# Stick-breaking stage: key parts in tile order, query rows turned between key blocks, head norms and head turns by halves

## The reference, cut to what matters

```python
k, v = split(rms_norm_2(h, kv_norm) @ w_kv)         # 256 x 1024 each, 8 heads of 128
k = rms_norm_2(k, k_norm)                           # per head of 128
q = rms_norm_2(rms_norm_2(h, ln_mix) @ w_q, q_norm) * 128 ** -0.5
z = q @ k.T                                         # per head, keys before the query only
A[t, s] = sigmoid(z[t, s]) * prod(1 - sigmoid(z[t, j]) for s < j < t)
h = h + (A @ v) @ w_out
```

## Time and profile before

| what | value |
|---|---|
| median of 3 runs | 1352.71 us (1350.2 to 1352.77) |
| the profiled execution | 1354.37 us, span 1352.7 us |
| TensorE busy | 1283.1 us, 95% of the span |
| DVE busy | 766.8 us, 57% |
| ACT busy | 610.7 us, 45% |
| POOL busy | 77.6 us, 6% |
| DMA | 212.26 MB, 157 GB/s over the span |

### The profile page before, as it was taken

One profiled execution on the slowest core, in us unless ns is written; L12 is line 12 of the kernel. 1 busy time (PEld: TensorE's weight loads), 2 busy tenths in 40 slices (PEclk: granted clock), 3 DMA queues, 4 the chain that ended last, 5 costly groups with the idle time before them and its releaser, 6 DMA issues.

```text
span 1352.7 us, 16268 instructions
## 1 busy us (share of the span) xinstructions
PE 1283.1 (95%) x6667; PEld 1086.9 (80%) x6667; DVE 766.8 (57%) x852; ACT 610.7 (45%) x743; POOL 77.6 (6%) x125
## 2 busy tenths in 40 slices
PE   8999999988999998999799999999979889999997
PEld 6888888987788887999598788888768777888886
DVE  4655436974655545587874655544656516554444
ACT  5444336644444434556303544442545735444323
POOL 1000002001100002001101100000102001000001
PEclk9999999989999998999898999999989899999999
DMA  8865546330765562645100576554545315665530
GB/s 267 266 188 187 201 151 215 133 102 12 237 186 188 187 218 94 218 145 183 32 1 1 155 221 201 173 189 159 183 144 191 99 38 166 215 201 177 189 133 31
DMA packets 140138, 212.26 MB, mean 157 GB/s; under 512 B 10233, under 2 KB 101245, under 8 KB 140060
## 3 DMA queue, kind: packets, MB, share of 16 engines
q1 hardware_dynamic: 140064, 211.22, 48.0%
HBM read 210.14 MB, written 1.05 MB: 156 GB/s over the span
## 4 chain that ended last, share of the span: by engine, by line
PE 87%; DVE 6%; ACT 3%; issue 1%; POOL 1%; DMA 0%; SPq 0%; ACTq 0%; DVEq 0%
PE bank L1443 25%; PE bank L1445 25%; PE bank L1444 25%; DVE wlo L959 2%; PE bank L1819 2%; PE bank L1466 1%; PE bank L1568 1%; PE bank L1827 1%; DVE xTlo L980 1%; PE bank L1686 1%; PE bank L1835 1%; DVE X L1003 1%; ACT whi L375 1%; ACT xThi L396 1%; DVE y L1204 1%
## 5 line engine op out<-in xcount | busy, mean ns | idle before, releaser
L959 DVE TENSOR_TENSOR wlo<-raw,whi 128x2048 fp32r<-128x2048 f32 x190 | 434.1, 2291 | 295.9 <-ACT whi L375 295.7
L375 ACT ACTIVATE whi<-raw 128x2048 fp32r<-128x2048 f32 x190 | 362.1, 1913 | 227.0 <-PE bank L1445 219.7
L1443 PE MATMUL bank<-whi,xThi 128*128 128x512 f32 x1024 | 408.8, 399 | 20.9 <-DVE xTlo L980 8.8
L1445 PE MATMUL bank<-whi,xTlo 128*128 128x512 f32 x1024 | 402.2, 393 | 0.0
L1444 PE MATMUL bank<-wlo,xThi 128*128 128x512 f32 x1024 | 401.9, 393 | 0.0
L1443 PEld LDWEIGHTS bank<-whi,xThi 128*128 128x128 f32 x1024 | 194.4, 190 | 66.1 <-DVE xTlo L980 9.4
L1445 PEld LDWEIGHTS bank<-whi,xTlo 128*128 128x128 f32 x1024 | 194.1, 190 | 41.5
L1444 PEld LDWEIGHTS bank<-wlo,xThi 128*128 128x128 f32 x1024 | 194.6, 190 | 38.7
L1443 PE MATMUL bank<-whi,hThi 128*128 128x512 f32 x352 | 138.1, 392 | 0.0
L1445 PE MATMUL bank<-whi,hTlo 128*128 128x512 f32 x352 | 137.1, 390 | 0.0
L1444 PE MATMUL bank<-wlo,hThi 128*128 128x512 f32 x352 | 137.0, 389 | 0.0
(11 more groups left out here) (375 smaller groups left out, 1222.6 us busy)
## 6 DMA issues: line engine op xcount, KB each, us to landing
raw<-in_ffn_w_dram SPq DMA_DIRECT2D x176, 256.0 KB, 4.0
raw<-in_ffn_w_in_dram SPq DMA_DIRECT2D x176, 256.0 KB, 3.9
raw<-in_ffn_w_dram SPq DMA_DIRECT2D x22, 1024.0 KB, 5.0
raw<-in_ffn_w_out_dram SPq DMA_DIRECT2D x22, 1024.0 KB, 4.9
raw<-in_gdn_w_in_dram SPq DMA_DIRECT2D x16, 1024.0 KB, 5.4
raw<-in_w_in_dram SPq DMA_DIRECT2D x10, 1024.0 KB, 5.2
raw<-in_ple_w_gate_dram SPq DMA_DIRECT2D x8, 1024.0 KB, 5.0
raw<-in_w_kv_dram SPq DMA_DIRECT2D x8, 1024.0 KB, 6.3
```

Of the source, the lines that this page charges most:

```text
L375: act.activation(whi[w % SPLIT][:], raw[w % RAW][:], ACT.Copy).then_inc(w_hi, 1)
L959: dve.tensor_tensor(wlo[w % SPLIT][:], raw[w % RAW][:], whi[w % SPLIT][:].bitcast(F32), ALU.subtract).then_inc(w_lo, 1)
L1443: pe.matmul(psum, lhs[0], rhs[0], start=start, stop=False, skip_group_check=True)
L1445: return pe.matmul(psum, lhs[1], rhs[0], start=False, stop=stop, skip_group_check=True)
```

## The change

`ahead` becomes 4 for "kv". TensorE does the four key slots on the first tile (n7's second turn before the last of them), then on the second tile, with the two turns of n8 before the third and the fourth part. DVE scales both tiles for n8 straight after n7. Squares, sums, roots and head norms are done for a half (512 columns, four heads) of both tiles as soon as the half is there; `sq_s` is used in two parts. Head turns go by halves too: both key halves before query block s+6, the first query half before s+8, the second after it. Bank 4 takes the first tile's turn and bank 5 the second's, where it was the half. Splits are placed anew between these steps. The computation is unchanged. The diff, with repeated signatures left out:

```diff
@@ -258,7 +258,7 @@
             arrived.append(total[w % RAW])
 
         def ahead(follows):
-            return {"up1": 3, "up2": 3, "up3": 3, "ple_g0": 4, "ple_g1": 4}.get(follows, 2)
+            return {"up1": 3, "up2": 3, "up3": 3, "ple_g0": 4, "kv": 4, "ple_g1": 4}.get(follows, 2)
 
         FIRST, PIECES = 2, 4
 
@@ -686,19 +686,19 @@
                                              ACT.Copy)
                     ins.then_inc(sem("s_kqv"), 1)
 
-                def squares(i):
+                def squares(i, b):
                     for t in range(NT):
-                        if 2 * i + t:
-                            act.wait_ge(sem("s_kss"), 2 * i + t)
-                        act.wait_ge(sem("s_kqv"), 2 * i + 2)
-                        act.activation(sq_s[:], kn[:, t, :], ACT.Square).then_inc(sem("s_sq"), 1)
-
-                def turned_heads(i, dst):
+                        n = 4 * i + 2 * b + t
+                        if n >= 2:
+                            act.wait_ge(sem("s_kss"), n - 1)
+                        act.wait_ge(sem("s_kqv"), 2 * i + b + 1)
+                        act.activation(sq_s[:, t * 512:(t + 1) * 512], kn[:, t, b * 512:(b + 1) * 512], ACT.Square).then_inc(sem("s_sq"), 1)
+
+                def turned_heads(i, b, dst):
                     for t in range(NT):
-                        for b in range(2):
-                            act.wait_ge(sem("s_kT"), 4 * i + 2 * t + b + 1)
-                            act.activation(dst[:, 4 * b:4 * b + 4, t * P:(t + 1) * P],
-                                           bank[4 + b][:].rearrange("p (k c) -> p k c", k=4), ACT.Copy).then_inc(sem("s_kT_in"), 1)
+                        act.wait_ge(sem("s_kT"), 4 * i + 2 * b + t + 1)
+                        act.activation(dst[:, 4 * b:4 * b + 4, t * P:(t + 1) * P],
+                                       bank[4 + t][:].rearrange("p (k c) -> p k c", k=4), ACT.Copy).then_inc(sem("s_kT_in"), 1)
 
                 def exp_abs(heads):
                     for h in heads:
@@ -720,30 +720,34 @@
 
                 norm(7, WIDE.index("ple_g0"), "kv", before=gate)
                 split(s + 1 + SPLIT)
+                turn_hi("n8", 0, xThi2)
                 act.wait_ge(w_used, s + 2)
                 evacuate(0, kn)
                 split(s + 2 + SPLIT)
-                norm(8, WIDE.index("ple_g0"), None, xThi2)
+                turn_hi("n8", 1, xThi2)
+                squares(0, 0)
                 split(s + 3 + SPLIT)
                 act.wait_ge(w_used, s + 4)
                 evacuate(1, kn)
-                split(s + 4 + SPLIT)
-                squares(0)
+                squares(0, 1)
                 split(s + 5 + SPLIT)
                 act.wait_ge(w_used, s + 6)
                 act.wait_ge(sem("s_rows"), 2)
                 evacuate(2, kn)
+                squares(1, 0)
+                for b in range(2):
+                    turned_heads(0, b, skT)
                 split(s + 7 + SPLIT)
                 act.wait_ge(w_used, s + 8)
+                act.wait_ge(sem("s_rows"), 4)
                 evacuate(3, kn)
-                turned_heads(0, skT)
-                split(s + 8 + SPLIT)
-                squares(1)
+                squares(1, 1)
+                turned_heads(1, 0, sqT)
                 split(s + 9 + SPLIT)
                 act.wait_ge(w_used, s + 10)
                 evacuate(4, vs)
+                turned_heads(1, 1, sqT)
                 split(s + 10 + SPLIT)
-                turned_heads(1, sqT)
                 exp_abs(range(6))
                 ln(range(6))
                 split(s + 11 + SPLIT)
@@ -927,8 +931,10 @@
                 select(sbig[:], ALU.is_ge, -BIG, -1, [[1, P]], -1)
                 select(neg_tri[:], ALU.is_ge, 0.0, 0, [[-1, P]], 1).then_inc(did("s_masks"), 1)
                 for i in range(2):
-                    for t in range(NT):
-                        root(krs[:, i, t, :], kms[:, i, t, :], kss[:, i, t, :], P, ("s_kss", "s_krs"), 2 * i + t + 1)
+                    for b in range(2):
+                        for t in range(NT):
+                            h = slice(4 * b, 4 * b + 4)
+                            root(krs[:, i, t, h], kms[:, i, t, h], kss[:, i, t, h], P, ("s_kss", "s_krs"), 4 * i + 2 * b + t + 1)
 
             norm(0)
             mixer1()
@@ -1319,26 +1325,27 @@
                     dve.tensor_tensor(X[:, t, :], X[:, t, :], gate_s[:, t, :], ALU.add).then_inc(sem("x_ready"), 1)
                 return add_gated
 
-            def head_norm(i, t, g_):
-
-                dve.wait_ge(sem("s_krs"), 2 * i + t + 1)
-                v = kn[:, t, :].rearrange("p (h c) -> p h c", h=H2)
-                w = xs[:, t, :].rearrange("p (h c) -> p h c", h=H2)
-                if i:
-                    dve.wait_ge(sem("s_kT"), 4)
-                else:
-                    dve.wait_ge(sem("turn_T"), 4 * turn("n8") + 4)
-                step(dve.tensor_tensor(w, v, krs[:, i, t, :].unsqueeze(2).broadcast_to([P, H2, P]), ALU.mult))
-                dve.tensor_tensor(w, w, head_gain[:, g_:g_ + 1, :].broadcast_to([P, H2, P]), ALU.mult).then_inc(sem("s_rows"), 1)
+            def head_norm(i, b, g_):
+
+                for t in range(NT):
+                    dve.wait_ge(sem("s_krs"), 4 * i + 2 * b + t + 1)
+                    v = kn[:, t, b * 512:(b + 1) * 512].rearrange("p (h c) -> p h c", h=4)
+                    w = xs[:, t, b * 512:(b + 1) * 512].rearrange("p (h c) -> p h c", h=4)
+                    if i:
+                        dve.wait_ge(sem("s_kT"), 2 * b + 2)
+                    else:
+                        dve.wait_ge(sem("turn_T"), 4 * turn("n8") + 4)
+                    step(dve.tensor_tensor(w, v, krs[:, i, t, 4 * b:4 * b + 4].unsqueeze(2).broadcast_to([P, 4, P]), ALU.mult))
+                    dve.tensor_tensor(w, w, head_gain[:, g_:g_ + 1, :].broadcast_to([P, 4, P]), ALU.mult).then_inc(sem("s_rows"), 1)
 
             def mixer3(add):
                 s = first["kv"]
 
-                def head_sums(i):
+                def head_sums(i, b):
                     for t in range(NT):
-                        dve.wait_ge(sem("s_sq"), 2 * i + t + 1)
-                        dve.tensor_reduce(kss[:, i, t, :], sq_s[:].rearrange("p (h c) -> p h c", h=H2), AX_X, ALU.add)\
-                           .then_inc(sem("s_kss"), 1)
+                        dve.wait_ge(sem("s_sq"), 4 * i + 2 * b + t + 1)
+                        dve.tensor_reduce(kss[:, i, t, 4 * b:4 * b + 4], sq_s[:, t * 512:(t + 1) * 512].rearrange("p (h c) -> p h c", h=4),
+                                          AX_X, ALU.add).then_inc(sem("s_kss"), 1)
 
                 def softplus(heads):
                     for h in heads:
@@ -1348,19 +1355,25 @@
                         dve.tensor_tensor(sab[:, h, :], sab[:, h, :], smask[:], ALU.mult).then_inc(sem("sb_sp"), 1)
 
                 norm(7, "kv", before=add)
+                for t in range(NT):
+                    norm_scale(8, t)
+                dve.tensor_scalar(head_gain[:, QG, :], head_gain[:, QG, :], P ** -0.5, None, ALU.mult).then_inc(did("s_qg"), 1)
+                split(s + 1 + SPLIT)
+                turn_lo("n8", 0, xThi2, xTlo2)
                 split(s + 2 + SPLIT)
-                norm(8, None, xThi2, xTlo2)
+                turn_lo("n8", 1, xThi2, xTlo2)
+                head_sums(0, 0)
+                head_norm(0, 0, KG)
                 split(s + 4 + SPLIT)
-                head_sums(0)
-
-                dve.tensor_scalar(head_gain[:, QG, :], head_gain[:, QG, :], P ** -0.5, None, ALU.mult).then_inc(did("s_qg"), 1)
-                for t in range(NT):
-                    head_norm(0, t, KG)
+                head_sums(0, 1)
+                head_norm(0, 1, KG)
+                split(s + 6 + SPLIT)
+                dve.wait_ge(*once("s_qg"))
+                head_sums(1, 0)
+                head_norm(1, 0, QG)
                 split(s + 8 + SPLIT)
-                head_sums(1)
-                dve.wait_ge(*once("s_qg"))
-                for t in range(NT):
-                    head_norm(1, t, QG)
+                head_sums(1, 1)
+                head_norm(1, 1, QG)
                 split(s + 10 + SPLIT)
                 dve.wait_ge(*once("s_masks"))
                 softplus(range(6))
@@ -1898,18 +1911,17 @@
             def mixer3():
                 s = first["kv"]
 
-                def head_turn(i):
+                def head_turn(i, b):
                     for t in range(NT):
-                        pe.wait_ge(sem("s_rows"), 2 * i + t + 1)
-                        for b in range(2):
-                            if i == 0 and t == 0:
-                                pe.wait_ge(sem("turn_lo"), 4 * turn("n8") + 4)
-                            if 4 * i + 2 * t + b - 1 > 0:
-                                pe.wait_ge(sem("s_kT_in"), 4 * i + 2 * t + b - 1)
-                            for k in range(4):
```

(43 more changed lines are left out.)

## The result

| | before | changed |
|---|---|---|
| median | 1352.8 us (1350.2 to 1356.4) | 1346.1 us (1340.1 to 1348.0) |
| ratio | | 0.9941, 95% interval 0.9916 to 0.9967 |
| profiled span | 1352.7 us | 1346.0 us |
| the stage, from n7's first turn to the value block s+10 | 89.9 us (972.06 to 1061.96) | 81.8 us (973.48 to 1055.31) |

A second set of runs of the changed kernel gave 1347.5 us, ratio 0.9957 (0.9940 to 0.9974). The forecast was 1342.5, range 1338.3 to 1347.6: faster, as said, but by 6.7 us in the medians instead of 10.2 (5.3 in the second set; the ratios, which are taken over all runs, say 8.0 and 5.8). The stage itself is 8.1 us shorter.

What follows compares the result with a forecast made beforehand. TensorE bounds the kernel, with 12.8 us idle and 7.8 slow within reach. Full-clock gain 12.4 less 2.2 for slow clock gives 10.2 us: median 1342.5, inner range 1341 to 1345, stated range 1338.3 to 1347.6.

Steps and rivals of the forecast that it cites:

- rival B: Head chains: a four-column root costs what an eight-column one does, chain 7.15 us, kernel 1348.4; chance 0.18 with mixtures.
- signs of being wrong: Half chain over 7 us, more than one turn ending in 1.2 GHz, or no key-turn wait (gain 14 us or more).
- (1): Splits four slots ahead for "kv": ACT's sum of squares 0.1 us later, n7's second scaling moves from 982.44 to 984.65.
- (2): First eight parts tile by tile: idle 8.31 becomes 2.6, 5.0 slow work goes; with the splits ahead worth 10.7 us.
- (3): Head chains by halves: four-column root 1.0 us, half chain 5.9; some 2 us more DVE work, 1 more ACT.
- C: Rival, head chains: a half chain costs what a whole one does, 10.0 us, kernel slower at 1357.1; chance 0.04.
- (4): Where chains lie: idle 2.0 and 1.7 us in second key turn, 1.1 and 0.75 in the last; 12.4 us full-clock gain.
- (5): Clock behind the second key turn's new wait: 1.2 GHz costs 2.2 us; the waits of 1.1 and 0.75 harmless.
- the new pair: Two new waits in the second key turn, 2.0 and 1.7 us: 3.7 idle in 4.2, taken as leading to slow clock.
- by idle times: Cross-check of the full-clock gain: 20.6 us idle and slow, less 8.15 idle remaining, gives the same 12.4.
- A: Rival: full clock throughout, also behind the key turn's new wait; gain 12.4 us, kernel 1340.3; chance 0.22.
- D: Rival: tile order and splits ahead only shift their waits; the remaining terms alone act and give nothing, 1353; chance 0.06.

Runs made afterwards that it cites:

- n7_scaling: Changed kernel with DVE's scaling of n7's second tile ahead of the second of two splits: stage 81.62 us, median 1345.6, ratio to before 0.9933.
- order_only: Changed kernel with squares, sums, roots, head norms and head turns on whole tiles as before: stage 79.68 us, median 1344.5, ratio to before 0.9934.
- turns_late: Changed kernel with both turns of n8 behind the eight key parts instead of between them: stage 84.42 us, median 1348.1, ratio to before 0.9965.
- warm_after: Changed kernel with never-read idle matmuls filling waits of the key turns and last turn: stage 77.68 us, median 1343.8, ratio to before 0.9925.
- halves_only: Changed kernel with the old order of first parts and n8, ahead left at 2, halves kept: stage 89.09 us, median 1353.6, ratio to before 1.0002.
- last_chain: Changed kernel with DVE norming the second query half ahead of the split of s+11: stage 79.53 us, median 1347.5, ratio to before 0.9948.
- warm_before: Kernel before the change with never-read idle matmuls in five TensorE waits: stage 82.80 us, median 1347.3, ratio to before 0.9959.
- key_turn: Changed kernel, second key half normed ahead of splits s+6 and s+7, key-turn banks emptied first: stage 75.93 us, median 1344.5, ratio to before 0.9924.
- all_moves: Changed kernel with the edits of key_turn, last_chain and n7_scaling together: stage 75.46 us, median 1341.1, ratio to before 0.9899.
- all_moves_2: all_moves plus the first query half normed ahead of the split of s+9: stage 74.02 us, median 1341.0, ratio to before 0.9902.

## Why the prediction was right, and where not

The way was right, and the time lies inside the stated range, for the second set by 0.1 us only. Part of that is luck: 1346.1 is above the inner range of 1341 to 1345, and the range reached to 1347.6 because of rival B (roots of four columns as dear as those of eight), which the rows refute. One of the prediction's own signs of being wrong also came: more than one turn ended in 1.2 GHz, the key turn and the last one. The layout at full clock was right; the price of the clock was not.

**(1), right, with one step missed.** The sum of squares started at 981.86, which is 980.45 by the clock of before: 0.1 late, as said. Missed: two wlo stood on DVE while POOL took n7's root. I had let POOL stand still beside DVE's products in the head chains but not here; the root took 2.48 and DVE's scaling came 0.5 late, so 0.5 of TensorE's idle ahead of the turn became 0.91. The experiment n7_scaling shows the cause: with the second wlo behind the scaling the root is 0.55.

**(2), right.** In the part up to the query block: idle 1.30, 0.91, 0.76 against 1.3, 0.5, 0.8 forecast; clock 1.00 throughout; the query block at 1003.8 against 1003.3. With order_only the part is worth 10.2 us, forecast 10.7. The covering of n8's turns is the larger part of what the query block gains (turns_late).

**(3), right.** Root 1.01 against 1.0, chain 5.8 against 5.9. Rivals B and C fall with these rows.

**(4), right in place, off in one split.** The first wait of the key turn came as 2.12 for 2.0, its successor as 0.78 for 1.7: by the clock of before the third group of transposes began 0.8 later than forecast and ran 0.3 longer (0.91 where full clock takes 0.63), while the rows came only 0.3 later (1020.98 less 1.41, against 1019.3). The last turn's waits came as 1.04 and 0.69 against 1.1 and 0.75.

**(5), this is the term that was mis-sized.** Two stretches of slow clock, not one, and 4.15 us instead of 2.2. warm_after shows how right the rest was: with the same real starts and full clock its stage is 77.68 us, and the prediction had laid it out as 77.5 (1049.6 less 972.06), so 12.2 us at full clock for the forecast 12.4; of the 0.46 lost by the root 0.3 came back behind the query block. Less 4.15 this is the 8.07 measured. The first slow stretch cost 2.46 against 2.2. The second I had called harmless, without a reason of its own: 1.04 and 0.69 idle with four transposes between, 1.73 in all. Behind it the scores took 5.62 instead of 3.95, in four profiles (changed twice, halves_only, n7_scaling). warm_after and last_chain, in which that wait is filled or shortened, both have them at 3.95; so does turns_late with the wait as it was, so it is a likely cause and not a sure one.

The ground for the first stretch was weaker than it looked. I called the new pair slow because it was denser than the old one, and a single 2.12 harmless by the earlier trace rows. In halves_only a single 2.12 with eight transposes behind it led to 0.50 as well, and in turns_late the same did not. What makes the difference no run shows. And 7.8 us for the slow stretches of before were 7.1 (warm_before), so "by idle times" gave 12.4 only because 0.7 too much clock made up for 0.7 too little work.

**Rivals.** A was against the rows: the clock did fall at the new wait. D is refuted: (1) and (2) bring 10.2 alone. What the working implied and the text said in one sentence, that (3) to (5) exchange their waits, is what halves_only shows (0.0002 in the ratio). It went further than that: on top of the tile order the halves cost 2.15 us in the stage. Behind the query block waits of 4.63 us and 4.15 of slow clock stand against 4.49 and 2.6 in order_only (its last turn and scores are those of before), which is 1.7 of it; 0.5 stays open, of which 0.28 is the slow third group. It is a comparison of single profiles, and with scores as fast as in turns_late little of it would be left. The medians don't settle it (1344.5 against 1346.1 and 1347.5, intervals overlapping).

**The median** lies 3.6 us above the forecast, of which the stage explains 2.1. The rest is most likely in where the clock fell ahead of the stage: there the profiles lie 9 us apart in code that is the same, and the runs of the changed kernel span 8 us at mean granted clocks of 0.979 to 0.987, the longest with the lowest. In which of the earlier stages these falls come stays open.

## What to carry to other kernels

Reorder so that the matmuls that need only what is there cover each hand-over (scale, turn, copy, subtract); the halves of a chain bring nothing when bulk work of 2.3 us a piece stands ahead of them in the same in-order queue, and moving that work behind the chain brought 5.9 us in the stage, 1.6 by shorter waits and the rest because no slow clock followed them. Price a wait of TensorE with the slow clock behind it: filling 9 us of waiting with idle matmuls, with nothing else moved, was worth 7.1 us of the stage, against 10.2 for the reordering. And compare such changes by the stage's own length in the profile, which repeated to 0.01 us in two profiles of one kernel, beside the run times, which scatter by 5 to 13. Look at the clock in it too: a slow stretch that stays away is worth 1.7 to 2.5 us here, with no edit to thank for it.

## What the runs showed of the hardware

The granted clock fell behind waits whose sum over a short stretch was only 1.73 us (1.04, four transposes, 0.69), in four profiles of five that have them; in turns_late it stayed at 1.00. It did not fall behind a single wait of 1.28 (key_turn, last_chain and both all_moves). A wait of 2.12 followed by real work stayed at full clock in the earlier trace rows. In the key turn the four transposes behind it were slow in both profiles of the changed kernel and in last_chain (0.91, 0.85, 0.84) and not in n7_scaling (0.63); eight in a row were fast in halves_only and turns_late (1.12 and 1.11), with slow matmuls behind them in the first only.

Behind the stage the same code has the same waits in all 13 profiles, and the clock differs. Behind a single wait of 2.93 ahead of the suffix sums it fell in nine and stayed up in four, here in the changed kernel and in n7_scaling, and the way to the next turn took 8.1 us or 6.5:

```profile
1083.10:1089.10 6.00, 6.00 (x34) 0.72 0.00 0
```

```profile
1082.00:1088.00 6.00, 5.77 (x44) 1.00 0.00 0
```

A little later the waits of 0.69, 1.07 and 1.5 led to slow transposes in four (1.62 to 1.73 for eight: last_chain, warm_after, turns_late, all_moves_2) and not in the other nine (1.16 or 1.17).

POOL's root of one column took 0.55 us alone and 2.48 with DVE's second wlo beside it: it began at 984.06, the two wlo ran from 981.64 to 986.13 at 2.3 us each, and it ended 0.4 later. By the Trainium skill, "SBUF — State Buffer", section on the two separate sides, a DVE instruction with two SBUF inputs excludes a GpSimd (POOL) one that reads SBUF, the memory that the two share; this trace agrees, and shows that one may stand still through the whole of a 2.3 us subtraction.
